# A mixture-of-experts tail on one core: the last expert tile unrolled, its up projection behind the down of the tile in front, and the token sums split between engines

## The reference

```python
h = rmsnorm(x, p['g_pre2']) * (1 + scale2) + shift2
# hier_moe: top-1 group, then top-2 experts inside it; gate holds two weights a token
for e in range(N_EXPERTS):                      # 16 experts
    a = jax.nn.silu(t @ p['w_eg'][e]) * (t @ p['w_eu'][e])
    y = y + gate[:, e:e + 1] * (a @ p['w_ed'][e])
x = x + gate2 * rmsnorm(y, p['g_post2'])
```

## Time and profile before

| | us |
|---|---|
| median of 3 runs (750.51, 754.04, 753.33) | 753.33 |
| the profiled execution | 752.38 |
| its span, from the first instruction to the last | 750.6 |
| TensorE busy in the span | 682.0 (91%) |
| VectorE busy | 489.9 (65%) |
| ScalarE busy | 420.3 (56%) |
| GpSimd busy | 72.6 (10%) |
| mean rate of all DMAs | 263 GB/s |
| mean granted TensorE clock | 0.957 of full |

### The profile page before, as it was taken

One profiled execution on the slowest core, in us unless ns is written; L12 is line 12 of the kernel. 1 busy time (PEld: TensorE's weight loads), 2 busy tenths in 40 slices (PEclk: granted clock), 3 DMA queues, 4 the chain that ended last, 5 costly groups with the idle time before them and its releaser, 6 DMA issues.

```text
span 750.6 us, 10815 instructions
## 1 busy us (share of the span) xinstructions
PE 682.0 (91%) x3523; PEld 537.7 (72%) x3523; DVE 489.9 (65%) x694; ACT 420.3 (56%) x626; POOL 72.6 (10%) x120
## 2 busy tenths in 40 slices
PE   3899999999999998989974969999999999999894
PEld 1466556579899986757864858888888888877651
DVE  2546433226554655664458858999999999888938
ACT  4542222224343545775343348887888888888833
POOL 1020101129400000000000600000000000000050
PEclk9899999999999998999975979999999999999988
DMA  9935666659952240300427599999999999999883
GB/s 338 387 132 196 225 225 204 213 165 359 400 160 89 75 141 27 113 1 15 183 74 263 224 347 398 398 398 398 399 398 398 398 398 398 398 398 398 348 301 147
DMA packets 92759, 197.54 MB, mean 263 GB/s; under 512 B 7811, under 2 KB 21176, under 8 KB 92724
## 3 DMA queue, kind: packets, MB, share of 16 engines
q1 hardware_dynamic: 81200, 163.08, 59.5%
q0 software_dynamic: 8224, 25.61, 9.2%
q10 hardware_dynamic: 3302, 8.43, 2.8%
HBM read 166.64 MB, written 30.44 MB: 263 GB/s over the span
## 4 chain that ended last, share of the span: by engine, by line
PE 62%; DMA 14%; DVE 8%; ACT 5%; SPq 4%; issue 4%; POOL 2%; POOLq 0%; ACTq 0%; DVEq 0%
PE ps L1652 14%; PE ps L1463 8%; PE ps L1672 7%; PE ps L1513 6%; PE ps L1499 6%; DMA raw_ring<-in_w_exp_down 5%; PE ps L1500 4%; PE ps L1393 3%; PE ps L1361 3%; DMA raw_ring<-in_w_in 2%; DMA qkv_mem<-in_w_exp_gate 2%; DVE split_ring L1147 2%; PE ps L1554 2%; PE ps L1529 2%; SPq L422 2%
## 5 line engine op out<-in xcount | busy, mean ns | idle before, releaser
L1652 PE MATMUL ps<-split_ring,split_rows 128*128 128x512 f32 x768 | 179.9, 393 | 1.3 <-DVE split_ring L1147 1.3
L1147 DVE TENSOR_TENSOR split_ring<-qkv_mem,split_ring 128x1024 fp32r<-128x1024 f32 x128 | 148.8, 1219 | 26.1 <-ACT split_ring L789 25.5
L1652 PEld LDWEIGHTS ps<-split_ring,split_rows 128*128 128x128 f32 x768 | 143.1, 188 | 31.7 <-DVE split_ring L1147 2.7
L789 ACT CAST split_ring<-qkv_mem 128x1024 fp32r<-128x1024 f32 x128 | 127.0, 1054 | 17.8 <-ACT catT_mem L813 9.3
L1499 PE MATMUL ps<-split_rows,split_ring 128*128 128x384 f32 x288 | 87.7, 345 | 0.8 <-DVE catT_mem L1065 0.4
L1672 PE MATMUL ps<-split_ring,split_rows 128*128 128x512 f32 x360 | 85.6, 393 | 0.0
L1500 PE MATMUL ps<-split_rows,split_ring 128*128 128x256 f32 x288 | 80.5, 279 | 0.0
L1147 DVE TENSOR_TENSOR split_ring<-raw_ring,split_ring 128x1024 fp32r<-128x1024 f32 x64 | 75.3, 1220 | 2.6 <-ACT split_ring L789 2.0
L1672 PEld LDWEIGHTS ps<-split_ring,split_rows 128*128 128x128 f32 x360 | 66.5, 188 | 13.1
L1463 PE MATMUL ps<-split_ring,split_rows 128*128 128x512 f32 x288 | 70.0, 396 | 0.0
L907 DVE TENSOR_TENSOR split_ring<-raw_ring,split_ring 128x1024 fp32r<-128x1024 f32 (+1 forms) x36 | 39.6, 1102 | 44.0 <-ACT split_ring L579 43.5
(11 more groups left out here) (282 smaller groups left out, 877.5 us busy)
## 6 DMA issues: line engine op xcount, KB each, us to landing
qkv_mem<-in_w_exp_gate SPq DMA_DIRECT2D x64, 512.0 KB, 12.3
qkv_mem<-in_w_exp_up SPq DMA_DIRECT2D x60, 512.0 KB, 11.1
raw_ring<-in_w_exp_down SPq DMA_DIRECT2D x60, 512.0 KB, 10.7
raw_ring<-in_w_mod SPq DMA_DIRECT2D x32, 512.0 KB, 4.9
expert_rows<-work POOLq DMA_DIRECT2D x54, 256.0 KB, 9.5
qkv_mem<-in_w_mod SPq DMA_DIRECT2D x16, 512.0 KB, 11.4
catT_mem<-expert_rows SPq DMA_DIRECT2D x16, 512.0 KB, 12.8
expert_rows<-catT_mem ACTq DMA_DIRECT2D x15, 512.0 KB, 6.6
```

The lines of the kernel that those rows point to most:

```text
L789: nc.scalar.copy(spl[:, moe_split_slot(tile, j, r), 0, :], moe_raw(tile, j, r)).then_inc(S["hi"], 1)
L1147: tt(spl[:, slot, 1, :], moe_raw(tile, j, r), spl[:, slot, 0, :].bitcast(F32), ALU.subtract).then_inc(S["lo"], 1)
L1652: ins = mm(ps[:, j, :], xS[:, s, k, :], spl[:, slot, m, (k % 2) * N:(k % 2 + 1) * N], start=(k == 0 and s + m == 0), stop=(k == KC - 1 and ...
```

## The change

The loop is one turn shorter (`rest` is the number of pairs less two), and its last two tiles, 14 and 15, are written out behind it. Tile 14 is as in the loop. For tile 15 the order is gate of 15, down of 14, up of 15, transposes of its activations, last down; SP, ScalarE and VectorE follow the same order. The rows of a tile 16 are no longer loaded, transposed and split. The rows of tile 14 are copied and written by ScalarE behind its casts of the up weights of tile 15.

In the end phase GpSimd starts its gathers for blocks 0 to 2 without waiting for the third group of weight quarters, and waits for it before block 3 (the buffers of the gathered rows are assigned anew). ScalarE, in VectorE's place, copies the second half of the last tile's rows. For blocks 0, 1 and 4 VectorE itself adds the gathered sum and the PSUM row (`z_rows`) in place of TensorE's identity matmul. For blocks 0 to 3 GpSimd adds x; block 4 stays with VectorE. ScalarE loads its table for the root with a dummy instruction ahead of the gathers. One semaphore per block for the second load of x is merged into the first.

```diff
+        GATE_UP_DOWN, LAST_ORDER = (0, 1, 2), (0, 2, 1)
+        BY_MATMUL, BY_ADD = (2, 3), (0, 1, 4)
@@ sync
-            with sp.Fori(0, later) as i:
+            with sp.Fori(0, rest) as i:
                 tile_in((i, 2))
                 tile_in((i, 3))
-            expert_quarters((later, 2), 0, w_ed, expert_of((later, 1)))
-            sp.wait_ge(S["lo"], moe_lo((later, 1), 1, 3))
+            tile_in((rest, 2))
+            e = expert_of((rest, 3))
+            expert_quarters((rest, 3), 0, w_eg, e)
+            expert_quarters((rest, 3), 1, w_ed, expert_of((rest, 2)))
+            expert_quarters((rest, 3), 2, w_eu, e)
+            expert_quarters((rest, 4), 0, w_ed, expert_of((rest, 3)))
+            sp.wait_ge(S["lo"], moe_lo((rest, 3), 1, 3))
@@ gpsimd
-            pool.wait_ge(S["xs_tr"], lin((rest, 2), 1, 1))
-            pool.wait_ge(S["lo"], moe_lo((rest, 1), 2, 3))
+            pool.wait_ge(S["lo"], moe_lo((rest, 3), 1, 3))
             pool.wait_ge(S["os_out0"], 16 * pairs + 16)
...
             for b in range(TB):
+                if b == 3:
+                    pool.wait_ge(S["lo"], moe_lo((rest, 3), 2, 3))
+                    pool.tensor_tensor(col(180), epsc, epsc, ALU.add).then_inc(S["pool_chain"], 1)
+                    pool.wait_ge(S["pool_chain"], 4)
...
+            for b in range(TB - 1):
+                pool.wait_ge(S["yscaled"], b + 1)
+                pool.tensor_tensor(yg(b, 1), yg(b, 0), x[:, b, :], ALU.add).then_inc(S["yadded"], 1)
@@ scalar
+            expert_tile((rest, 2))
+            last = (rest, 3)
+            split_expert(last, 0)
+            aT_hi((rest, 2))
+            out_rows((rest, 1))
+            split_expert(last, 1)
+            gate_act(last)
+            split_expert(last, 2)
+            out_rows((rest, 2))
+            for r in range(4):
+                act.wait_ge(S["dn_mm"], lin(last, 4, r - 3))
+                act.wait_ge(moe_sem((rest, 4), 0, r), moe_loaded((rest, 4), 0, r))
+                nc.scalar.copy(spl[:, moe_split_slot((rest, 4), 0, r), 0, :], moe_raw((rest, 4), 0, r)).then_inc(S["hi"], 1)
+            aT_hi(last)
+            nc.scalar.activation(col(184), epsc, ACT.Sqrt)
...
+            gated_row(0)
+            gated_row(1)
+            act.wait_ge(S["dn_last"], 2)
+            nc.scalar.copy(last_out[:, N:D], ps[:, 6, :]).then_inc(S["last_rows"], 1)
+            gated_row(2)
+            row_square(0)
+            gated_row(3)
+            row_square(1)
+            gated_row(4)
+            row_square(2)
+            row_square(3)
+            row_square(4)
@@ vector
+            split_lo_moe(last, 0)
+            aT_lo((rest, 2))
+            split_lo_moe(last, 1)
+            split_lo_moe(last, 2)
+            split_lo_moe((rest, 4), 0, (0, 1))
+            gated(last)
+            split_lo_moe((rest, 4), 0, (2,))
+            aT_lo(last)
+            split_lo_moe((rest, 4), 0, (3,))
...
+            def z_rows(b):
+                y = psf[:, LAST_BANKS[b] * N:LAST_BANKS[b] * N + D]
+                dve.wait_ge(S["z_mm_last"], BY_ADD.index(b) + 1)
+                dve.wait_ge(S["ysq"], b + 1)
+                tt(yg(b, 0), yg(b, 0), y, ALU.add).then_inc(S["z_rows"], 1)
...
             def row_out(b):
                 c = 1 if b == CTX else 0
-                y = psf[:, LAST_BANKS[b] * N:LAST_BANKS[b] * N + D]
+                y = psf[:, LAST_BANKS[b] * N:LAST_BANKS[b] * N + D] if b in BY_MATMUL else yg(b, 0)
                 dve.wait_ge(S["yrt"], b + 1)
                 link(nc.vector.reciprocal(rs4[:, b:b + 1], rt4[:, b:b + 1]))
-                link(stt(yg(b, 0), y, rs4[:, b:b + 1], gate2[:, c, :], ALU.mult, ALU.mult))
-                tt(yg(b, 1), yg(b, 0), x[:, b, :], ALU.add).then_inc(S["yout"], 1)
+                if b < TB - 1:
+                    stt(yg(b, 0), y, rs4[:, b:b + 1], gate2[:, c, :], ALU.mult, ALU.mult).then_inc(S["yscaled"], 1)
+                else:
+                    link(stt(yg(b, 0), y, rs4[:, b:b + 1], gate2[:, c, :], ALU.mult, ALU.mult))
+                    tt(yg(b, 1), yg(b, 0), x[:, b, :], ALU.add).then_inc(S["yout"], 1)
+            dve.wait_ge(S["dn_last"], 1)
+            nc.vector.tensor_copy(last_out[:, 0:N], ps[:, 5, :]).then_inc(S["last_half"], 1)
             row_sum(0)
             row_sum(1)
-            for b in range(TB):
-                if b + 2 < TB:
-                    row_sum(b + 2)
+            z_rows(0)
+            row_sum(2)
+            z_rows(1)
+            row_sum(3)
+            row_out(0)
+            row_sum(4)
+            z_rows(4)
+            for b in range(1, TB):
                 row_out(b)
@@ tensor
-            last_down((later, 1), (later, 2))
+            expert_tile((rest, 2))
+            last = (rest, 3)
+            gate_up(last, (0,))
+            down((rest, 2), last, 1)
+            gate_up(last, (1,), LAST_ORDER)
+            a_transposes(last)
+            last_down(last, (rest, 4))
+            pe.wait_ge(S["last_half"], 1)
             last_add(0, 0)
             last_add(1, 0)
+            pe.wait_ge(S["last_rows"], 1)
+            last_add(0, 1).then_inc(S["z_mm_last"], 1)
+            last_add(1, 1).then_inc(S["z_mm_last"], 1)
             for b in range(2, TB):
                 if b == TB - 1:
-                    pe.wait_ge(S["yout"], 1)
+                    pe.wait_ge(S["z_rows"], 1)
                 last_add(b, 0)
-                last_add(b, 1)
-                row_add(b)
+                ins = last_add(b, 1)
+                if b in BY_ADD:
+                    ins.then_inc(S["z_mm_last"], 1)
+                else:
+                    row_add(b)
```

More of the change, by code:

```diff
@@ L141, in build @@
         x_in = [sem(f"x_in{b}") for b in range(TB)]
-        x_again = [sem(f"x_again{b}") for b in range(TB)]
-        S = {n: sem(n) for n in ("yg1 last_oh last_tr last_ev dn_last last_rows y_mm "
+        S = {n: sem(n) for n in ("yg1 z_mm_last z_rows last_half yscaled yadded last_oh last_tr last_ev dn_last last_rows y_mm "
             "stage_in cond_in vec_tr rope_in ck_in cv_in wr_in "
@@ L325, in build @@
         assert at[0] <= 1024
-        ymem = ([raw[:, n, :] for n in range(RAW)] + [qkv[:, 2048:3072], qkv[:, 3072:4096]]
-                + [catT_mem[:, n * D:(n + 1) * D] for n in (0, 1, 2, 4)])
+        ymem = [qkv[:, 2048:3072], qkv[:, 3072:4096]] + [catT_mem[:, n * D:(n + 1) * D] for n in (0, 1, 4, 2)] + [
+            raw[:, n, :] for n in range(RAW)]
         last_out = ostage[1]
@@ L778, in _, with split_expert @@
             h2T_out(4)
-            def split_expert(tile, j):
-                for r in range(4):
+            def split_expert(tile, j, quarters=range(4)):
+                for r in quarters:
                     if tile[0] is None and tile[1] == 0:
@@ L844, in _ @@
             expert_tile((None, 1))
-            later = act.value_load(steer[0:1, 30:31], min_val=NEXP // 2 - 1, max_val=MAX_PAIRS - 1)
-            with act.Fori(0, later) as i:
+            rest = act.value_load(steer[0:1, 29:30], min_val=NEXP // 2 - 2, max_val=MAX_PAIRS - 2)
+            with act.Fori(0, rest) as i:
                 expert_tile((i, 2))
                 expert_tile((i, 3))
-            split_expert((later, 2), 0)
-            aT_hi((later, 1))
-            out_rows((later, 0))
+            expert_tile((rest, 2))
[13 more added lines that the diff above has]
+            nc.scalar.activation(col(184), epsc, ACT.Sqrt)
             def gated_row(b):
@@ L1141, in _, with split_lo_moe @@
                 second_norm(i)
-            def split_lo_moe(tile, j):
-                for r in range(4):
+            def split_lo_moe(tile, j, quarters=range(4)):
+                for r in quarters:
                     dve.wait_ge(S["hi"], moe_lo(tile, j, r))
@@ L1283, in _ @@
             expert_tile((None, 1))
-            later = dve.value_load(steer[0:1, 30:31], min_val=NEXP // 2 - 1, max_val=MAX_PAIRS - 1)
-            with dve.Fori(0, later) as i:
+            rest = dve.value_load(steer[0:1, 29:30], min_val=NEXP // 2 - 2, max_val=MAX_PAIRS - 2)
+            with dve.Fori(0, rest) as i:
                 expert_tile((i, 2))
                 expert_tile((i, 3))
-            split_lo_moe((later, 2), 0)
-            aT_lo((later, 1))
+            expert_tile((rest, 2))
[9 more added lines that the diff above has]
+            split_lo_moe((rest, 4), 0, (3,))
             dve.wait_ge(S["gate2_in"], 32)
-            later_out = dve.value_load(steer[0:1, 31:32], min_val=NEXP // 2, max_val=MAX_PAIRS)
-            dve.wait_ge(S["os_out1"], 16 * later_out)
+            pairs = dve.value_load(steer[0:1, 31:32], min_val=NEXP // 2, max_val=MAX_PAIRS)
+            dve.wait_ge(S["os_out1"], 16 * pairs)
             def row_sum(b):
@@ L1641, in x_transposes, with gate_up @@
                 ins.then_inc(S["xs_tr"], 1)
-            def gate_up(tile):
-                for j in range(2):
+            def gate_up(tile, parts=(0, 1), order=GATE_UP_DOWN):
+                for j in parts:
```

(8 more changed lines are left out.)

46 lines of the change are left out of this document (19 added, 27 removed).

## The result

| | before | after |
|---|---|---|
| median, us (8 runs each, same chip) | 753.67 (750.51 to 755.78) | 760.02 (757.84 to 761.9) |
| the profiled execution | 752.38 | 759.11 |
| its span | 750.6 | 757.3 |
| mean granted clock | 0.957 | 0.953 |
| GpSimd busy | 72.6 | 85.9 |

The ratio after to before is 1.0086, interval 1.0067 to 1.0105: 6.5 us slower. The prediction was 752.8, range 747 to 756, with "slower" the least likely side.

The account below looks back on a forecast made before the run. DMA was taken to bound the loop, then a TensorE, write, gather and VectorE chain. The tail's 4.7 us gain nearly all went to GpSimd's additions: span 750.1 against 750.6, so 753.33 - 0.5 = 752.8, range 747 to 756.

Parts of the forecast that it names:

- the tile order with its numbers (703.9, 705.6, 712.8): Loop exit: tile 14's down ends at 703.9, its write is issued at 705.6, the last down starts at 712.8.
- the DMA-bound loop gives next to nothing: Loop over expert tiles: DMA engines full at 399 GB/s, each tile keeps its bytes; zero counted, bounds 0 and 1.3 us.
- The clock fell again before the last down: Last down: lower clock expected again after shorter idle time, ending at 721.3; at full clock 718.5.
- GpSimd's addition, bounded between 0.9 and 4.6 and taken at 2.3: End phase: each two-input addition of x for blocks 0 to 3 on GpSimd takes 2.3 us.
- The exclusion of VectorE's and GpSimd's two-operand instructions: End phase: two-SBUF-operand VectorE operations and GpSimd's additions exclude one another; span 749.9 to 751.2, 748.7 without; forecast case, chance 0.40.
- VectorE's last addition near 743 to 744.5: Sign listed for the end phase: when VectorE's final addition would be seen if the forecast held.
- its own sum with the exclusion: End of the kernel: span taken as 750.1, between 749.9 with GpSimd first and 751.2 with VectorE first.
- the span ends at 750.6, 3.0 us later: Way out: from the last output's issue at 747.59 to the end of the span, read from the earlier trace.
- 1.4 where block 4's sum waits for TensorE: End phase: VectorE stalls 1.4 us before block 4's sum, while TensorE works from 725.4 to 734.3.
- the first weighting 7.2 us behind a release at 711.7: Gathers: tile 14's write lands at 711.7, first gathered block at 718.9; ScalarE's copy then done at 723.6.
- End: 742.8, against 747.55: Summing in the end phase: VectorE has 16.2 us of work plus stalls of 0.5 and 1.4, ending 4.7 us earlier.
- The slower case that I named: Rival, chance 0.10: GpSimd additions stretched beside VectorE; at 3.5 us each GpSimd ends at 751.0, measured time 758.1.

Follow-up runs that it names:

- b_pool_late: The kernel before plus one one-column GpSimd addition that waits for block 3's output; ratio 1.0036 to the kernel before, span 754.0 us.
- b_pool_wait: The kernel before plus only a wait for block 3's output at the end of GpSimd's program; span 755.7 us from a single execution.
- a_dve_adds: The changed kernel with all additions of x on VectorE; ratio 1.0027 to the kernel before, span 754.1 us.
- a_z4_late: The changed kernel with VectorE's sum of block 4 behind the products of blocks 1 and 2; ratio 1.0056 to the kernel before, end phase 34.5 us.
- t_act_copy: a_tiles_only with ScalarE copying the last tile's second half behind block 1's weighting; ratio 1.0002 to the kernel before, end phase 35.5 us.
- t_sums: a_tiles_only with VectorE summing blocks 0, 1 and 4, block 4 as late as possible; ratio 0.9993 to the kernel before, end phase 35.7 us.
- a_tiles_only: The changed kernel with the end phase of before, except that ScalarE's early table load stayed in; ratio 0.9941 to the kernel before, span 748.8 us.
- t_gate2_late: a_tiles_only with SP's two gate2 rows held back until tile 14's write has landed; ratio 0.9934 to the kernel before, span 745.0 us.
- t_pool01: a_tiles_only with GpSimd adding x for blocks 0 and 1 alone; ratio 0.9956 to the kernel before, end phase 31.1 us.
- the joint one: t_gate2_late and t_pool01 combined: late gate2 rows and GpSimd adding x for blocks 0 and 1; ratio 0.9946 to the kernel before.

## Why the prediction was wrong

**Right:** the tile order with its numbers (703.9, 705.6, 712.8), and that the DMA-bound loop gives next to nothing (the 24 matmuls of the down projection of tile 14 start at 697.80, those that stood in their place at 698.18). The clock fell again before the last down in this profile (7.35 instead of 8.5 is a clock that came back sooner inside it); that is the likelier case and no rule, since in four of the eleven profiles with this order it stayed full. GpSimd's addition, bounded between 0.9 and 4.6 and taken at 2.3, measured 2.32. The exclusion of VectorE's and GpSimd's two-operand instructions, drawn from the earlier trace rows in one direction, holds in both: GpSimd's additions took 3.32 and 3.33 where VectorE's two-operand instruction came first, VectorE's 2.92 and 3.25 where GpSimd did. The Trainium skill's rule (SBUF — State Buffer, "SBUF: two separate sides") agrees with these rows. The estimate of 2.25 us, worked out from its 4497 ns at 2048 columns (GPSIMD Engine Reference, "Elementwise — side-by-side cycle accounting"), agrees with 2.32. Three signs were to show the prediction wrong (additions under 1.7, the write landing after 714, a stall where the engines leave the loop); none came true, and it was wrong all the same. Its sign "VectorE's last addition near 743 to 744.5" does not fit its own sum with the exclusion, which issues the last output at 746.9 to 748.2.

**Wrong, 4.5 us:** the term that closes the sum, "the span ends at 750.6, 3.0 us later" than the last output's issue. 3.0 was read from the earlier trace rows, in a kernel where GpSimd had been through for 22 us. The change makes GpSimd work to within 1.1 us of the last output, and its own way out of 8.6 us becomes the end: b_pool_late and b_pool_wait show it with nothing else changed. No row of before shows that distance. Without it the changed kernel would be about where a_dve_adds is, 1.0027: still no faster than before.

**Wrong, 2.7 us:** the last output's issue (749.78 against 747.1, the 750.1 less 3.0). The step that failed is the stall of "1.4 where block 4's sum waits for TensorE", which was to be done at 734.3. TensorE was done at 738.01, 3.7 later, in two parts. 2.1 is ScalarE's copy (725.70, not 723.6): I set the first weighting 7.2 us behind a release at 711.7, and it came 8.5 behind 712.54. Of that 1.2, 0.8 is the exclusion again, at a place that I had not priced: GpSimd's one-column addition ahead of the gathers took 0.97 us instead of 0.19 and ended 0.05 behind VectorE's last subtraction.

```profile
712.32 1.22 DVE L1185 TENSOR_TENSOR split_ring<-qkv_mem,split_ring 128x1024 fp32r<-128x1024 f32 x1
...
712.62 0.97 POOL L544 TENSOR_TENSOR small<-small 128x1 f32<-128x1 f32 x1 [280.36 <-DMA expert_rows<-catT_mem]
```

The other 1.6 is the clock: from the copy to the end of block 4's product TensorE took 12.3 us where the forecast had 10.7, and the 8 matmuls alone took 5.23 from their start to that of the next instead of 3.44 (2 x 1.72), of which the forecast had 0.2 to spare elsewhere. The forecast priced no lower clock there, because its own numbers left no long gap: last down to 721.3, 1.7 for the first halves, copy at 723.6, which is 0.6 us of idle time. The gap became 4.14 because the last down ended 1.4 sooner (719.9) and the copy 2.1 later. Blocks 1 to 3, which stand behind that sum in VectorE's order, were scaled from 740.66 on instead of 737.1; 0.8 of the 3.5 was absorbed in the exclusion that followed. a_z4_late shows the stall's share: 2.7 us of end phase.

**Wrong in the account of the parts:** "End: 742.8, against 747.55", VectorE through 4.7 us sooner, counts the three sums as 3.75 us of work and the copy as 0.6 us on ScalarE, without what other engines wait for them but the 0.5 and 1.4. By themselves copy and sums cost 3.2 and 3.4 us of end phase (t_act_copy, t_sums), and the four additions gave nothing net. VectorE ended at 749.76. The slower case that I named (it decides from additions of 3.3 us on; at 3.5, GpSimd through at 751.0) is not what happened: two of the four took 3.3 with their waits, but GpSimd was through at 748.67, and what followed it was 8.6 us and not 4.4. The side was right for another reason.

**Open:** what GpSimd does in its 8.6 us; what decides whether the clock falls before the last down; and how the copy and the sums share the 5.0 us that they cost together. The medians put a_tiles_only 10.9 us under the changed kernel, the spans of the profiled executions 8.5; the ratios are uncertain by 0.19 and 0.25%, 1.4 and 1.9 us.

Four versions beat both kernels: a_tiles_only, t_gate2_late, t_pool01 and the joint one. They have in common the new tile order, the table load ahead of the gathers, and copy and sums as they were.

## What to carry to other kernels

Before an engine gets work near the end, look at when it was through before, and price its way out of the program, not only the work. Work moved off the engine that sets the end counts only if nothing on that engine waits longer for it: look at what stands behind the operand in the other engine's order (here a copy of 0.6 us behind a gather), and at what a gap does to TensorE's clock. A version that is to isolate one half of a change must be read in its own trace: here a_tiles_only still had the table load of the other half. An in-order engine should meet an operand that comes late as late in its order as it can.

## What the runs showed of the hardware

- From GpSimd's last instruction to the end of the span are 8.6 us (five kernels, 8.6 to 8.7), 8.9 from a wait alone. The kernels whose GpSimd is through early end 3.0 us after the last output's issue.
- GpSimd's addition of two SBUF operands of 128x1024 fp32 takes 2.32 us, VectorE's 1.22. Beside a VectorE instruction with two SBUF inputs one waits for the whole of the other (3.32; 2.92 and 3.25). A one-column addition on GpSimd does too: 0.97 to 1.19 us beside VectorE's subtraction, 0.19 to 0.21 away from it. Beside a VectorE product with one PSUM input neither is longer (2.32 each, 1.28).
- A 512 KB write landed after 6.5 us with two broadcast rows issued 5 us before it and after 4.1 without them (t_gate2_late and the joint version alike).
- Between the short matmul groups of the end phase TensorE's granted clock fell to the lower level behind gaps of 3.4 to 5.8 us (8 matmuls in 5.40 to 6.72, 4 in 3.62 to 3.78, where 4 take 1.88 at full clock), and stayed full behind gaps of 0.4 to 1.6 (4 in 1.98). The last down, behind 1.48 us of idle time, had it at both levels: 5.7 us in four profiles, 7.1 to 7.4 in seven.
